# Sample attention in a hybrid decoder layer: order of the last attention unit, of one loading queue, and of the gate loads

## The reference, cut to what matters

```python
u = rmsnorm(x) @ w_in                       # q, k, v of 3 groups; z, x/B/C, dt; gates
for gi, (window, dil) in enumerate(((128, 1), (512, 4), (2048, 16))):
    # prompt: causal dilated window attention over its own keys
    # sample: the 8 queries read cached keys and values, then the new ones
    s = einsum('bshe,bskhe->bshk', q, keys) * ATTN_SCALE
    p, lse = softmax(s);  o = einsum('bshk,bskhe->bshe', p, values)
    new_kv = concat(past, kv_new)[-rows:]   # an output: the cache moved on by 8 rows
a_out = sum_g softmax_g(lse) * o_g
y = ssd branch (gated, normed)
mixed = (sigmoid(gate_a) * (a_out @ w_attn_out) + sigmoid(gate_b) * (y @ w_ssd_out)) @ w_out
x = x + rmsnorm(mixed);  x = x + rmsnorm(swiglu_ffn(rmsnorm(x)))
```

## Time and profile before

| | us |
|---|---|
| median of three runs | 3084.24 (3080.14 to 3092.83) |
| the profiled execution | 3089.35 |
| its span | 3087.6 |
| PE busy | 2914.9 (94%) |
| DVE busy | 1373.2 (44%) |
| POOL busy | 810.3 (26%) |
| ACT busy | 799.7 (26%) |

### The profile page before, as it was taken

The page is one execution under the profiler, slowest core; times in us unless marked ns, Lnnn a source line. Parts: engine busy times, 40 slices in busy tenths (PEclk is TensorE's granted clock), DMA queues, the critical chain, the costliest instruction groups (busy, mean ns, idle before and its releaser), DMA issues.

```text
span 3087.6 us, 45803 instructions
## 1 busy us (share of the span) xinstructions
PE 2914.9 (94%) x17443; PEld 2701.9 (88%) x17443; DVE 1373.2 (44%) x2374; ACT 799.7 (26%) x1945; POOL 810.3 (26%) x552
## 2 busy tenths in 40 slices
PE   7999999999999999999999985679889999999997
PEld 6989998899999889998989973339889999999997
DVE  5475556546554753222222324667752222222234
ACT  5442144125314420232323232212330000000003
POOL 2332323233322323211212101023222323232322
PEclk9999999999999999999999997889999999999999
DMA  5534344334424342112122247784101111111111
GB/s 172 172 106 149 100 137 135 92 127 133 157 64 150 120 134 86 51 35 74 54 58 77 52 134 191 245 249 141 36 22 48 41 48 41 48 41 48 41 52 63
DMA packets 330966, 302.47 MB, mean 98 GB/s; under 512 B 27280, under 2 KB 297152, under 8 KB 329192
## 3 DMA queue, kind: packets, MB, share of 16 engines
q1 hardware_dynamic: 246328, 243.09, 25.9%
q10 hardware_dynamic: 84456, 56.93, 6.2%
HBM read 250.81 MB, written 102.91 MB: 115 GB/s over the span
## 4 chain that ended last, share of the span: by engine, by line
PE 88%; DVE 4%; DMA 2%; issue 2%; ACT 1%; POOL 1%; SPq 1%; ACTq 0%; DVEq 0%; POOLq 0%
PE ps L2081 24%; PE ps L2083 23%; PE ps L2082 23%; PE ps L2342 2%; PE ps L2226 2%; PE ps L2363 2%; PE ps L2284 1%; PE ps L2281 1%; PE ps L2354 1%; PE ps L2233 1%; PE ps L2452 1%; PE ps L2438 1%; PE ps L2232 1%; DMA wraw<-in_w_out_dram 1%; DVE smvraw L1836 1%
## 5 line engine op out<-in xcount | busy, mean ns | idle before, releaser
L2081 PE MATMUL ps<-hH,wH 128*128 128x368 f32 (+1 forms) x2208 | 743.9, 337 | 6.3 <-POOL wL L747 2.1
L2083 PE MATMUL ps<-hH,wL 128*128 128x368 f32 (+1 forms) x2208 | 725.6, 329 | 0.0
L2082 PE MATMUL ps<-hL,wH 128*128 128x368 f32 (+1 forms) x2208 | 724.9, 328 | 0.0
L745 POOL CAST wH<-wraw 128x1024 fp32r<-128x1024 f32 (+1 forms) x181 | 202.8, 1120 | 1599.5 <-PE ps L2083 1248.6
L2081 PEld LDWEIGHTS ps<-hH,wH 128*128 128x128 f32 x2208 | 417.4, 189 | 44.2 <-issue 35.7
L747 POOL TENSOR_TENSOR wL<-wraw,wH 128x1024 fp32r<-128x1024 f32 (+1 forms) x181 | 447.5, 2472 | 14.5
L2082 PEld LDWEIGHTS ps<-hL,wH 128*128 128x128 f32 x2208 | 417.8, 189 | 0.5
L2083 PEld LDWEIGHTS ps<-hH,wL 128*128 128x128 f32 x2208 | 416.9, 189 | 0.0
L2081 PE MATMUL ps<-mH,wH 128*128 128x368 f32 (+1 forms) x1128 | 371.7, 330 | 8.9 <-DVE mL L1955 7.7
L2082 PE MATMUL ps<-mL,wH 128*128 128x368 f32 (+1 forms) x1128 | 370.6, 329 | 0.0
L2083 PE MATMUL ps<-mH,wL 128*128 128x368 f32 (+1 forms) x1128 | 370.3, 328 | 0.0
(11 more groups left out here) (386 smaller groups left out, 4618.1 us busy)
## 6 DMA issues: line engine op xcount, KB each, us to landing
wraw<-in_w_in_dram SPq DMA_DIRECT2D x92, 512.0 KB, 4.1
wraw<-in_w_up_dram SPq DMA_DIRECT2D x44, 512.0 KB, 3.8
ssdcr<-cum_scr ACTq DMA_DIRECT2D x32, 512.0 KB, 5.2
out_dram<-in_cache_kv_w_dram SPq DMA_DIRECT2D x16, 960.0 KB, 5.6
smkraw<-in_cache_kv_w_dram SPq DMA_DIRECT2D x45, 256.0 KB, 6.9
wraw<-in_w_down_dram SPq DMA_DIRECT2D x22, 512.0 KB, 3.7
smkraw<-in_cache_kv_w_dram SPq DMA_DIRECT2D x9, 1024.0 KB, 6.0
smvraw<-in_cache_kv_w_dram SPq DMA_DIRECT2D x35, 256.0 KB
```

The costliest lines, as they stand in the source:

```text
L745: pool.tensor_copy(hi, a).then_inc(w_hi, 1)
L2081: pe.matmul(dst, hi, cols(mH[:, k, :], c), start=k == 0, stop=False)
L2082: pe.matmul(dst, hi, cols(mL[:, k, :], c), start=False, stop=False)
L2083: last = pe.matmul(dst, lo, cols(mH[:, k, :], c), start=False, stop=k == kt - 1)
```

## The change

- The last unit's helpers are in another order: query_rows at step 0, new_scores at step 2, new_rows at 4, 6 and 8 on TensorE; on ScalarE behind steps 1, 3, 5, 7 and 8. The order of the output DMAs is held by waits on kvn_out: scores wait for the query DMA, rows 0 for the score DMA, and so on.
- n_scr has another layout, token by head by sequence by (group, key), so that each sequence's own scores of a token and head are 24 neighbours; ScalarE's copies put them so.
- SP: load_q(0) directly behind load_k(0), newS behind the sends of unit (3,1), load_k(1) next, then atok, the sends of unit (3,2), load_new(0), merge_load(3).
- Gates: the loop loads only column block 0; blocks 1 and 2 follow as two pairs of larger DMAs behind the two halves of accm; mix(c) waits for its own block.
- ScalarE: rows_in(b) ahead of expo(b+1).
- TensorE waits for the score copies inside scores(0), behind the first key transposes.

```diff
-        n_scr = scratch("n_scr", [NS, NG, HEADS, NS])
+        n_scr = scratch("n_scr", [NS, HEADS, DB, NG * DS])
...
-        nsc = at("nsc", [NS, NG, NJ, 2, NS], off=WS + 16384)
+        nsc = at("nsc", [NS, HEADS, DB, NG, DS], off=WS + 16384)
... SP
                     load_k(0)
+                    sp.wait_ge(kvn_out, 16)
+                    load_q(0)
                     sp.wait_ge(mk_out, 16)
                     sp.dma_start(maskS[:, :], mk_scr.unsqueeze(0).to_broadcast([HEADS, DS, 1176])).then_inc(mS_in, 16)
                     load_v(0)
                     send_unit(NJ - 1, 1)
+                    sp.wait_ge(kvn_out, 16 * 2)
+                    for b in range(DB):
+                        sp.dma_start(newS[:, b, :], n_scr[DS * b:DS * b + DS, :, b, :].rearrange("q h n -> h q n")).then_inc(mS_in, 16)
+                    sp.wait_ge(k_fill, 8)
+                    sp.wait_ge(k2_done, 1)
+                    load_k(1)
                     sp.wait_ge(a_out, 16 * 2)
                     for j in range(2):
                         sp.dma_start(atok[:, :, j * P:(j + 1) * P], a_scr[j]).then_inc(at_in, 16)
+                    send_unit(NJ - 1, 2)
                     sp.wait_ge(kvn_out, 16 * 8)
-                    load_q(0)
-                    for b in range(DB):
-                        own = slice(DS * b, DS * b + DS)
-                        sp.dma_start(newS[:, b, :].rearrange("p (g k) -> p g k", g=NG),
-                                     n_scr[own, :, :, own].rearrange("q g h k -> h q g k")).then_inc(mS_in, 16)
                     load_new(0)
-                    send_unit(NJ - 1, 2)
-                    sp.wait_ge(k_fill, 8)
-                    sp.wait_ge(k2_done, 1)
-                    load_k(1)
                     merge_load(NJ - 1)
...
                     def load_gate(k, m):
-                        sp.dma_start(gates[k][:, m, :], gate_scr[k, m]).then_inc(gates_in, 16)
+                        sp.dma_start(cols(gates[k][:, m, :], 0), cols(gate_scr[k, m], 0)).then_inc(gates_in, 16)
+
+                    def load_gates(c):
+                        sp.wait_ge(gates_in, 16 * (2 * KD + 2 * (c - 1)))
+                        for k in range(2):
+                            sp.dma_start(cols3(gates[k], c), cols3(gate_scr[k].rearrange("m p n -> p m n"), c)).then_inc(gates_in, 16)
...
                     sp.dma_start(accm[:, 0:4, :], ba_scr[:, 0:4, :]).then_inc(ba_in[0], 16)
+                    load_gates(1)
                     sp.wait_ge(aL_ready, NT + 1)
                     sp.dma_start(accm[:, 4:8, :], ba_scr[:, 4:8, :]).then_inc(ba_in[1], 16)
+                    load_gates(2)
... ScalarE
             def new_rows(gr):
-                act.wait_ge(kvn_ps, gr + 1)
-                if gr:
-                    act.wait_ge(kvn_out, 32 * gr)
+                act.wait_ge(kvn_ps, gr + 5)
+                act.wait_ge(kvn_out, 32 * gr + 32)
...
             def new_scores():
-                act.wait_ge(kvn_ps, NG + 2)
+                act.wait_ge(kvn_ps, 2)
+                heads = nsc[:, :, :, :, :].rearrange("p (j s) b g k -> p s g j b k", s=2)
                 for s in range(2):
-                    act.copy(nsc[:, 0:2, :, s, :], G[1 + s][0:NS, :].rearrange("p (g j k) -> p g j k", g=2, j=NJ)).then_inc(kvn_ev, 1)
-                act.wait_ge(kvn_ps, NG + 4)
-                act.copy(nsc[:, 2, :, :, :].rearrange("p j s k -> p (j s k)"), G[0][0:NS, :]).then_inc(kvn_ev, 1)
-                act.wait_ge(kvn_ev, 2 * NG + 4)
-                act.dma_start(n_scr, nsc[:, :, :, :, :].rearrange("p g j s k -> p g (j s) k")).then_inc(kvn_out, 16)
+                    for gr in range(2):
+                        ins = act.copy(heads[:, s, gr], G[1 + s][0:NS, gr * 256:gr * 256 + 256].rearrange("p (j b k) -> p j b k", j=NJ, b=DB))
+                    ins.then_inc(kvn_ev, 1)
+                act.wait_ge(kvn_ps, 4)
+                act.copy(nsc[:, :, :, 2, :], G[0][0:NS, :].rearrange("p (h b k) -> p h b k", h=HEADS, b=DB)).then_inc(kvn_ev, 1)
+                act.wait_ge(kvn_ev, 4)
+                act.wait_ge(kvn_out, 16)
+                act.dma_start(n_scr.rearrange("t h b n -> t (h b n)"), nsc[:, :, :, :, :].rearrange("p h b g k -> p (h b g k)")).then_inc(kvn_out, 16)
...
-                    elif i in (2, 4, 6):
-                        new_rows(i // 2 - 1)
-                    elif i == 7:
+                    elif i == 1:
                         query_rows()
-                    elif i == 8:
+                    elif i == 3:
                         new_scores()
+                    elif i in (5, 7, 8):
+                        new_rows((i - 5 + 1) // 2)
...
                 keys_in(b + 1)
                 probs_in(b)
+                rows_in(b)
                 expo(b + 1)
-                rows_in(b)
... VectorE
             def mix(c):
+                dve.wait_ge(gates_in, 16 * (2 * KD + 2 * c))
...
-            dve.wait_ge(gates_in, 16 * 2 * KD)
... TensorE
-                    if nxt is None and i in (1, 3, 5):
-                        new_rows(i // 2)
-                    if nxt is None and i == 6:
+                    if nxt is None and i == 0:
                         query_rows()
-                    if nxt is None and i == 8:
+                    if nxt is None and i == 2:
                         new_scores()
+                    if nxt is None and i in (4, 6, 8):
+                        new_rows(i // 2 - 2)
...
             def new_rows(gr):
-                for c in range(3) if gr == 0 else ():
-                    pe.wait_ge(g_free[c], U_SAM)
-                if gr:
-                    pe.wait_ge(kvn_ev, (1, 1, 4)[gr])
+                pe.wait_ge(kvn_ev, (4, 5, 8)[gr])
...
-            pe.wait_ge(kvn_ev, 2 * NG + 4)
...
                         pe.wait_ge(qb_ready, b + 1)
+                        if first:
+                            pe.wait_ge(kvn_ev, 2 * NG + 4)
```

More of the change, by code:

```diff
@@ L1170, in new_rows @@
             def new_rows(gr):
-                act.wait_ge(kvn_ps, gr + 1)
-                if gr:
-                    act.wait_ge(kvn_out, 32 * gr)
+                act.wait_ge(kvn_ps, gr + 5)
+                act.wait_ge(kvn_out, 32 * gr + 32)
                 for kv in range(2):
                     act.copy(kvn[:, kv, :], G[(2 * gr + kv) % 3][0:NS, :]).then_inc(kvn_ev, 1)
-                act.wait_ge(kvn_ev, 2 * gr + 2)
+                act.wait_ge(kvn_ev, 2 * gr + 6)
                 for kv in range(2):
@@ L1181, in query_rows @@
             def query_rows():
-                act.wait_ge(kvn_ps, NG + 1)
+                act.wait_ge(kvn_ps, 1)
                 act.copy(qrow, G[0][0:NS, :]).then_inc(kvn_ev, 1)
-                act.wait_ge(kvn_ev, 2 * NG + 1)
+                act.wait_ge(kvn_ev, 1)
                 act.dma_start(q_scr, qrow).then_inc(kvn_out, 16)
             def new_scores():
-                act.wait_ge(kvn_ps, NG + 2)
+                act.wait_ge(kvn_ps, 2)
+                heads = nsc[:, :, :, :, :].rearrange("p (j s) b g k -> p s g j b k", s=2)
                 for s in range(2):
-                    act.copy(nsc[:, 0:2, :, s, :], G[1 + s][0:NS, :].rearrange("p (g j k) -> p g j k", g=2, j=NJ)).then_inc(kvn_ev, 1)
-                act.wait_ge(kvn_ps, NG + 4)
-                act.copy(nsc[:, 2, :, :, :].rearrange("p j s k -> p (j s k)"), G[0][0:NS, :]).then_inc(kvn_ev, 1)
-                act.wait_ge(kvn_ev, 2 * NG + 4)
-                act.dma_start(n_scr, nsc[:, :, :, :, :].rearrange("p g j s k -> p g (j s) k")).then_inc(kvn_out, 16)
+                    for gr in range(2):
[6 more added lines that the diff above has]
+                act.dma_start(n_scr.rearrange("t h b n -> t (h b n)"), nsc[:, :, :, :, :].rearrange("p h b g k -> p (h b g k)")).then_inc(kvn_out, 16)
             def unit(j, gr, nxt, merge=None):
@@ L2366, in unit @@
                         mm.then_inc(pv_ready, 1)
-                    if nxt is None and i in (1, 3, 5):
-                        new_rows(i // 2)
-                    if nxt is None and i == 6:
+                    if nxt is None and i == 0:
                         query_rows()
-                    if nxt is None and i == 8:
+                    if nxt is None and i == 2:
                         new_scores()
+                    if nxt is None and i in (4, 6, 8):
+                        new_rows(i // 2 - 2)
             def query_rows():
-                pe.wait_ge(kvn_ev, 4)
+                for c in range(3):
+                    pe.wait_ge(g_free[c], U_SAM)
                 for j in range(NJ):
@@ L2380, in new_scores @@
             def new_scores():
-                pe.wait_ge(kvn_ev, 2 * NG)
                 def score(out, gr, j, s):
@@ L2392, in new_scores @@
                 mm.then_inc(kvn_ps, 1)
-                pe.wait_ge(kvn_ev, 2 * NG + 1)
+                pe.wait_ge(kvn_ev, 1)
                 for s in range(2):
@@ L2398, in new_scores @@
                     mm.then_inc(kvn_ps, 1)
-                    pe.wait_ge(kvn_ps, NG + 3 + s)
```

(8 more changed lines are left out.)

## The result

The changed kernel takes 3071.02 us (median of 10 runs, 3063.28 to 3077.81) against 3084.69 for the kernel before in the same series (10 runs): ratio 0.9949, 95% interval 0.9937 to 0.9962. Timed once more in a later series it took 3068.85 against 3088.2: 0.9935, 0.9923 to 0.9948. It is faster by 0.5 to 0.65%, some 14 to 19 us. The forecast was 28.5 us, or 3056 us.

What follows compares the result with a forecast made beforehand. The chain was taken as 88% TensorE, with its pauses between 1829 and 2085 winnable. Terms -14 - 0.5 - 10 - 4 = -28.5 us took the profiled 3089.35 to 3060.9, or 3056 against the median; range 3038 to 3077, own range 3048 to 3065.

Steps and rivals of the forecast that it cites:

- step 2: SP's load order at the front: keys 1 land 16 us earlier, keys 2 then wait; gain 14 us, bounds 5 to 20.
- step 4: TensorE's clock in the sample loop: half speed behind pauses goes, 1 us in four passes, 4 us; ends 0 and 8.
- step 6: The rest, newS pieces and w_attn_out splits beside DVE in sequence 6: worth 0 us, ends -3 and +3.
- step 3: ScalarE's output rows copied ahead of the exponential: sequences 2 to 5 gain 10 us, sequence 1 gains 0.5, sequence 0 nothing.
- Step 1: Order in the last attention unit: ScalarE starts the key copies at 1860.5 instead of 1868.05, 7 to 8 us earlier.
- Rival D: In the last unit, output DMAs take 17 us each and the kernel is 16 us slower, 3100; chance 0.06.
- Step 5: Gates loaded by column block: cost nothing, with 3 us of cover at accm; upper end 8 us.
- A: Loads bound the sample loop, which gives 4 us instead of 14: -18.5 us, 3066; chance 0.15.
- B: At the front, the merge load does not hold keys 2: -37 us, 3047; chance 0.17.
- C: The front gives only 5 us because keys 2 land at 1912, and the loop gives 4: 3075; chance 0.12.

Runs made afterwards that it cites:

- k2_first: The changed kernel with the merge load for head pair 3 issued behind keys 2 instead of ahead of them; 0.9941 of the kernel before.
- v7_first: The changed kernel with the last sequence's values loaded ahead of the last two w_attn_out tiles; 0.9925 of the kernel before, 0.9929 when timed again.

## Why the prediction was right in sign and too large

The measured 3071.02 us lie inside the range of 3038 to 3077 and outside the forecast's own 3048 to 3065. The wide range held because it was drawn around rivals too, and not because the terms were sized right: of 28.5 us came 13.7 in the first series and 19.4 in the later. The terms that failed are step 2's landing of keys 2, step 4's clock, step 6's zero, and what opens behind the pause that step 3 removes.

*Step 1, the unit's order: right.* Query rows were foretold near 1833 and issued at 1832.49; scores near 1838.5 and 1839.26, landed after 6.16 us (I took 6); ScalarE's key copies at 1860.5 and at 1862.26. Rival D needed four trips of 13 us each from issue to landing: the query rows took at most 5.3 us (SP's load that waits for them was issued at 1837.77), the score rows 6.16, rows 0 7.92, rows 1 2.72, and ScalarE waited 2.75, 3.79 and 3.47 us for them. D is out.

*Step 2, SP's order: right in kind, the term too large.* Keys 1 went ahead and TensorE's pause fell from 17.09 to 8.51 us. The foretold new wait for keys 2 is there, and they were issued at 1892.67 as I had said (near 1892). But their query rows landed 11.0 us behind their own issue, not 8.1, and the issue, query rows included, took 5.7 us, not 4.3: S2 gained 8.8 us, not 14. I had priced the merge load only by how long SP stands in it. Its 1.6 MB are also in the DMA engines ahead of keys 2. k2_first shows it: with keys 2 first their query rows land after 8.1 us, and S2 stands 6.6 us earlier. The Trainium skill (DMA: Bandwidth & Descriptors, Queues, rings and completion order) says that each engine takes the descriptors of a ring in order; by that the merge rows come first, and the trace agrees with its 11.0 us.

*Step 3, output rows first: right, and its 10 us are there; what opened behind it was not in the sum.* L2506 waits 0.76 us in each pass, as foretold, and over passes 2 to 5 (from S3 to S7) that is 10.05 us less. But the four passes shrank by 8.1 us together, where steps 3 and 4 had 14. TensorE's other pauses in them grew by 3.75 us: ahead of the first score product from 0.55 to 2.48 us in sum, ahead of the next key transposes from nothing to 1.73, of which 1.09 is the wait for the query rows of sequence 7, and 0.09 ahead of the probabilities. TensorE's busy time fell by 1.8 us. That is all of the 8.1.

The pause ahead of the first score product is ScalarE's copy of the transposed keys. TensorE waits 0.54 us for it once the ten transposes are fast, and waited 0.55 at the one place where they were fast before:

```profile
1957.07 0.40 PE L2449 MATMUL ps<-smkt,smqb 128*64 128x128 f32 x2 [0.55 <-ACT smkt L1245]
```

After the change, in the pass from S5, ScalarE itself waits for TensorE ahead of that copy, so there the exponential costs nothing:

```profile
1987.70 1.41 ACT L1255 COPY smkt<-ps 128x512 f32<-128x512 f32 x4 [0.30 <-PE ps L2441]
...
1988.78 0.40 PE L2454 MATMUL ps<-smkt,smqb 128*64 128x128 f32 x2 [0.54 <-ACT smkt L1255]
```

Only in the pass from S4, where TensorE waits 1.09 us, does the exponential, 1.28 us, stand directly ahead of the key copies and hold them up:

```profile
1966.17 1.28 ACT L1259 ACTIVATE sms<-sms,small 64x1176 f32<-64x1176 f32 x1 [0.85 <-DVE small L1822]
1967.45 1.36 ACT L1255 COPY smkt<-ps 128x512 f32<-128x512 f32 x4
```

In the second execution it does so in the passes from S5, S6 and S7 too (waits of 0.84 to 0.86 us). The terms at sequences 0 and 1 came out as said: nothing, and merge_exp(3) later, by 1.05 us.

*Step 4, the clock: the sign seen, the gain not.* I had 4 us. The busy time fell by 1.8 us, and the first score products wait 1.9 us longer, mostly for the key copies that the slow transposes had hidden: net nothing. The ten key transposes take 1.31 us from S4 on, as foretold, but 1.72 at S3 (2.39 in the second execution). The half speed did not go, it moved: in the pass from S4 the granted clock is 0.92, and the ten products with values take 6.17 us where they take 4.48 in the passes from S3 and S6. Over the four passes it was 0.96, 0.87, 0.89, 0.87 before and 0.91, 0.92, 0.92, 1.00 after. Where it falls differs between executions: in the second one those products took 4.48 in all four passes, and the stretch from 1975 to 1994 had 0.91. I had taken the slow transposes as the whole loss, when they were the place at which it showed.

*Step 5, gates: right.* 1.0001 alone. The second half of accm landed 8.5 us after its issue, and mix waited for no gate.

*Step 6: the term was not zero.* I gave the splits of w_attn_out and the last values 0, from -3 to +3. The last pass grew by 1.7 us in one execution and 2.1 in the other. In the second, VectorE's first addition met a split and took 3.94 us, and TensorE waited 3.89 us for the three additions; before, the first one ran undisturbed and TensorE waited 2.25:

```profile
2057.22 2.29 DVE L1836 TENSOR_TENSOR smvraw<-smvraw,smred 128x2048 f32<-128x2048 f32 x1 [0.24 <-DVE smred L1829]
```

The profiles of v7_first show 6 us to be had in that pass. A part that I priced at nothing had in it waits that the order of two loads decides. The Trainium skill (GPSIMD Engine Reference, Specifications) says that GpSimd shares its SBUF interfaces with VectorE, with contention for VectorE instructions that have two inputs in SBUF or run in a 2-port performance mode. The additions agree (2.60 us for one of 0.69). A copy of 24 columns, with one input, took 2.31 us instead of 0.16 beside a split in the first execution; whether it ran in such a mode no run shows.

*The rivals.* A, TensorE waiting for query rows in passes 3 to 7: only ahead of sequence 7, 1.09 us. B fell with the 7.93 us wait. C had S2 at keys 2 landing at 1912; they landed at 1908.7, half way between it and the forecast. So at the front the time lies half way between C and the forecast, by the mechanism of step 2. The loop gave 8.1 us, between A's 4 and the forecast's 14, and but for the 1.09 us not by A's mechanism: no rival had ScalarE's key copies or the clock that moves. That 3071 lies between A's 3066 and C's 3075 confirms neither.

The sum, again in profiled us from U: front -8.8 instead of -14.5, passes 2 to 5 -8.1 instead of -14, last pass +1.7, the rest -2.2 (the pass from S2 -0.4, and 1.8 behind P, no more than executions of the same code differ by there): -17.4.

## What to carry to other kernels

A load that is moved ahead moves the wait to the next load, and what is issued between them is paid twice: in the issuing engine's time (here keys 2 were issued 2.3 us later) and again in the issue and landing of what follows (1.4 and 2.9 us). Follow the queue until the first item with slack, and put the ones without slack ahead of all that has it; here moving the merge load, which had slack, behind keys 2 and values 1, which had none, won 6.3 us more in the median (3067.60 to 3061.34, of five and four runs). A pause removed on TensorE gives back its length less the pauses that open behind it (here 10.05 us less 3.75), and a slow clock seen at one instruction is not won when that instruction gets fast.

## What the runs showed of the hardware that was not expected

- Merge rows (three DMAs of 528 KB) took 2.01 us to issue into an empty queue, 10.09 and 6.92 behind a load of keys, 5.13 behind values. Query rows behind them landed in 11.0 us instead of 8.1.
- The clock's loss is not tied to one pause: with pauses of 0.76, 0.97 and 1.09 us in a pass, the granted clock was 0.92 in one pass and 1.00 in another of the same form.
- A subtraction on GpSimd that takes 2.34 us took up to 4.27 beside VectorE's additions, and an addition of 1.22 us took 3.14: both engines lose.
- Work ahead of the edit, the same in all kernels, ended between 1815.4 and 1826.4 us in the profiled executions. Only marks counted from there could be compared to a microsecond or two, and the stretch behind P still varied from 1000.8 to 1007.4.
